# State space angle tables: from GpSimd to VectorE, in ten parts between the remainders of a feed-forward layer

## The reference

```python
def hybrid_layer(x, g_mix, w_in, sinks, w_a, w_b, w_out, g_mlp, w_up, w_down):
    ...
    x = x + mixed @ w_out
    h2 = rmsnorm(x, g_mlp)
    x = x + jnp.square(jax.nn.relu(h2 @ w_up)) @ w_down
    return x

def s5_ssm(u, lam_re, lam_im, log_dt, b_re, b_im, c_re, c_im, d):
    ...
    dt = jnp.exp(log_dt.astype(f32))[:, None]
    mag = jnp.exp(lr * dt)
    ab_re = mag * jnp.cos(li * dt)
    ab_im = mag * jnp.sin(li * dt)
    ...
    _, _, xr, xi = lax.associative_scan(combine, (a_re, a_im, bu_re, bu_im), axis=1)
```

## Time and profile before

| | |
|---|---|
| median of 3 runs | 1128.41 us (1128.15 to 1132.17) |
| the profiled execution, its own time | 1132.87 us |
| its span, first to last instruction | 1131.1 us |
| TensorE matmul busy | 1056.7 us, 93% of the span |
| VectorE busy | 748.0 us, 66% |
| ScalarE busy | 507.5 us, 45% |
| GpSimd busy | 327.7 us, 29% |
| mean granted TensorE clock | 0.968 of full |

### The profile page before, as it was taken

How to read it: one execution, slowest core, us unless ns; L and a number is a source line. 1 busy time by engine, 2 the same in 40 slices (tenths; PEclk the granted TensorE clock), 3 DMA queues, 4 the chain that set the end, 5 groups by cost and what they waited for, 6 DMA issues and landing times.

```text
span 1131.1 us, 15013 instructions
## 1 busy us (share of the span) xinstructions
PE 1056.7 (93%) x6385; PEld 918.7 (81%) x6385; DVE 748.0 (66%) x745; ACT 507.5 (45%) x630; POOL 327.7 (29%) x174
## 2 busy tenths in 40 slices
PE   9899999999999999999999998758999999898687
PEld 7777888898999888777888987747988998897476
DVE  4777646565555557667466677998557584796764
ACT  5355544454444453555444533312457454532242
POOL 0430000000000004300000699997000094284641
PEclk9999999999999999999999998968999999898989
DMA  8444445555655554454454735323645534337222
GB/s 297 145 170 154 150 148 186 161 179 182 195 192 188 176 182 140 168 176 150 149 176 160 223 128 174 107 87 134 221 155 170 186 137 168 103 121 194 76 94 75
DMA packets 97316, 180.34 MB, mean 159 GB/s; under 512 B 8568, under 2 KB 13536, under 8 KB 97120
## 3 DMA queue, kind: packets, MB, share of 16 engines
q1 hardware_dynamic: 97072, 179.28, 48.2%
q10 hardware_dynamic: 176, 0.09, 0.0%
HBM read 175.98 MB, written 1.05 MB: 157 GB/s over the span
## 4 chain that ended last, share of the span: by engine, by line
PE 66%; DVE 17%; DMA 6%; ACT 5%; issue 4%; POOL 2%; SPq 0%; DVEq 0%; POOLq 0%; ACTq 0%
PE bank L677 20%; PE bank L680 19%; PE bank L679 19%; DVE w_lo L1467 9%; DMA raw<-in_w_in 5%; ACT w_hi L1125 4%; DVE arena L1596 2%; PE bank L782 1%; DMA raw<-in_o_w_in 1%; POOL arena L2058 1%; PE bank L1044 1%; PE bank L692 1%; POOL h_sb L2055 1%; PE bank L684 1%; DVE arena L522 1%
## 5 line engine op out<-in xcount | busy, mean ns | idle before, releaser
L1467 DVE TENSOR_TENSOR w_lo<-raw,w_hi 128x2048 fp32r<-128x2048 f32 (+1 forms) x159 | 415.8, 2621 | 272.5 <-ACT w_hi L1125 272.3
L1125 ACT ACTIVATE w_hi<-raw 128x2048 fp32r<-128x2048 f32 (+1 forms) x164 | 310.2, 1892 | 361.2 <-PE bank L680 187.5
L677 PE MATMUL bank<-hT_hi,w_hi 128*128 128x256 f32 x816 | 238.7, 293 | 27.4 <-DVE w_lo L1467 23.2
L679 PE MATMUL bank<-hT_lo,w_hi 128*128 128x256 f32 x792 | 229.0, 289 | 0.0
L680 PE MATMUL bank<-hT_hi,w_lo 128*128 128x256 f32 x792 | 228.9, 289 | 0.0
L677 PE MATMUL bank<-w_hi,hT_hi 128*128 128x512 f32 (+1 forms) x552 | 215.2, 390 | 11.9 <-ACT arena L1137 5.8
L680 PE MATMUL bank<-w_hi,hT_lo 128*128 128x512 f32 (+1 forms) x500 | 192.1, 384 | 0.0
L679 PE MATMUL bank<-w_lo,hT_hi 128*128 128x512 f32 (+1 forms) x500 | 191.8, 384 | 0.0
L677 PEld LDWEIGHTS bank<-hT_hi,w_hi 128*128 128x128 f32 x816 | 162.5, 199 | 32.4 <-DVE w_lo L1467 24.8
L679 PEld LDWEIGHTS bank<-hT_lo,w_hi 128*128 128x128 f32 x792 | 157.4, 199 | 0.4
L680 PEld LDWEIGHTS bank<-hT_hi,w_lo 128*128 128x128 f32 x792 | 156.9, 198 | 0.0
(11 more groups left out here) (299 smaller groups left out, 1237.8 us busy)
## 6 DMA issues: line engine op xcount, KB each, us to landing
raw<-in_w_in SPq DMA_DIRECT2D x44, 1024.0 KB, 5.1
raw<-in_w_up SPq DMA_DIRECT2D x32, 1024.0 KB, 5.3
raw<-in_w_down SPq DMA_DIRECT2D x32, 1024.0 KB, 5.1
raw<-in_e_w_in SPq DMA_DIRECT2D x12, 1024.0 KB, 5.1
raw<-in_o_w_in SPq DMA_DIRECT2D x10, 1024.0 KB, 5.2
raw<-in_w_b SPq DMA_DIRECT2D x8, 1024.0 KB, 5.0
raw<-in_w_out SPq DMA_DIRECT2D x8, 1024.0 KB, 5.1
raw<-in_w_a SPq DMA_DIRECT2D x4, 1024.0 KB, 5.1
```

The lines of the kernel that those rows point to most:

```text
L677: pe.matmul(dst, a_hi, b_hi, start=first, stop=False, skip_group_check=shared)
L679: pe.matmul(dst, a_hi, b_lo, start=False, stop=False, skip_group_check=shared)
L1125: act.activation(w_hi[:, p % SPLIT_RING, :, 0:n], raw[:, p % RAW_RING, :, 0:n], copy).then_inc(hi_ready, 1)
L1467: dve.tensor_tensor(w_lo[:, s, :, 0:n], raw[:, p % RAW_RING, :, 0:n], w_hi[:, s, :, 0:n].bitcast(F32), ALU.subtract).then_inc(lo_ready, 1)
```

## The change

The tables' work leaves GpSimd. `state_space_angles` shrinks to `state_space_turns`, which keeps the small tensors and raises a new semaphore `s5_turns`; it no longer waits for the arena. VectorE gets `state_angles(part)` with ten parts. The tables are made in two halves of 8 tiles (128 x 2048) with five stages each: stage 0 multiplies the time by the high part and finds the whole turns, stage 1 takes them off, stage 2 adds the low part, stage 3 takes whole turns off again, and stage 4 makes the cosine's angle as sin + 0.25 - (sin > 0.25). In groups f = 0 to 4 of the second layer, part 2f stands after the first two remainders of the group and part 2f + 1 after `mlp_square`. ScalarE's two sines move from the second block into groups 5 and 6 of the same layer, where ScalarE waits for both halves (`s5_angles` at 2). VectorE's wait for `s5_angles` ahead of `xg` is gone.

```diff
@@ scalar
                 for f in range(F_GROUPS):
                     step(p + DOWN_PIECE[f])
                     step(p + DOWN_PIECE[f] + 1)
+                    if l == DEPTH - 1 and f in (F_GROUPS - 3, F_GROUPS - 2):
+                        act.wait_ge(s5_angles, 2)
+                        table = (s5_sin, s5_cos)[f - (F_GROUPS - 3)][:, :, :].rearrange("p s t -> p (s t)")
+                        act.activation(table, table, ACT.Sin, scale=TWO_PI).then_inc(s5_tables, 1)
...
             act.activation(s5_small[:, 2, :], s5_small[:, 0, :], ACT.Exp).then_inc(s5_decay, 1)
-            act.wait_ge(s5_angles, 1)
-            act.activation(s5_sin[:, :, :].rearrange("p s t -> p (s t)"), s5_sin[:, :, :].rearrange("p s t -> p (s t)"),
-                           ACT.Sin, scale=TWO_PI).then_inc(s5_tables, 1)
...
-            act.activation(s5_cos[:, :, :].rearrange("p s t -> p (s t)"), s5_cos[:, :, :].rearrange("p s t -> p (s t)"),
-                           ACT.Sin, scale=TWO_PI).then_inc(s5_tables, 1)
@@ vector
+            def state_angles(part):
+
+                half, stage = divmod(part, 5)
+                tiles = range(half * S5_TILES // 2, (half + 1) * S5_TILES // 2)
+                at = slice(tiles[0], tiles[-1] + 1)
+                sin, cos, tmp = (v[:, at, :].rearrange("p s t -> p (s t)") for v in (s5_sin, s5_cos, s5_tmp))
+                order.settle()
+                if stage == 0:
+                    if half == 0:
+                        dve.wait_ge(s5_turns, 1)
+                    for i in tiles:
+                        order.mark(dve.tensor_scalar(s5_sin[:, i, :], tab("time"), s5_small[:, 3, i:i + 1], None, ALU.mult))
+                    order.settle()
+                    order.mark(dve.tensor_scalar(tmp, sin, ROUND, -ROUND, ALU.add, ALU.add))
+                elif stage == 1:
+                    order.mark(dve.tensor_tensor(sin, sin, tmp, ALU.subtract))
+                elif stage == 2:
+                    for i in tiles:
+                        order.mark(dve.scalar_tensor_tensor(out=s5_sin[:, i, :], in0=tab("time"), scalar=s5_small[:, 4, i:i + 1],
+                                                            in1=s5_sin[:, i, :], op0=ALU.mult, op1=ALU.add))
+                elif stage == 3:
+                    order.link(dve.tensor_scalar(tmp, sin, ROUND, -ROUND, ALU.add, ALU.add))
+                    order.mark(dve.tensor_tensor(sin, sin, tmp, ALU.subtract))
+                else:
+                    order.link(dve.tensor_scalar(tmp, sin, 0.25, None, ALU.is_gt))
+                    dve.scalar_tensor_tensor(out=cos, in0=sin, scalar=0.25, in1=tmp, op0=ALU.add, op1=ALU.subtract)\
+                       .then_inc(s5_angles, 1)
+                    dve.wait_ge(s5_angles, half + 1)
...
                 for f in range(F_GROUPS - 1):
                     step(p + DOWN_PIECE[f])
                     step(p + DOWN_PIECE[f] + 1)
+                    if l == DEPTH - 1 and f < 5:
+                        state_angles(2 * f)
                     if f + 2 < F_GROUPS:
                         step(p + UP_PIECE[f + 2])
                         step(p + UP_PIECE[f + 2] + 1)
                         mlp_square(l, f + 2)
+                    if l == DEPTH - 1 and f < 5:
+                        state_angles(2 * f + 1)
...
-                                dve.wait_ge(s5_angles, 1)
@@ gpsimd
-            def state_space_angles():
-
-                pool.wait_ge(out_free[1], (DEPTH - 1) * USES + USE_UP)
+            def state_space_turns():
+
...
-                for i in range(S5_TILES):
-                    order.mark(pool.tensor_scalar(s5_sin[:, i, :], tab("time"), s5_small[:, 3, i:i + 1], None, ALU.mult))
...
-                pool.tensor_tensor(s5_cos, s5_cos, s5_tmp, ALU.subtract).then_inc(s5_angles, 1)
+                pool.tensor_tensor(s[4], s[1], s[3], ALU.subtract).then_inc(s5_turns, 1)
+                pool.wait_ge(s5_turns, 1)
```

More of the change, by code:

```diff
@@ L394, in build_program @@
         s5_decay = sem("s5_decay")
+        s5_turns = sem("s5_turns")
         s5_angles = sem("s5_angles")
```

15 lines of the change are left out of this document (1 added, 14 removed).

## The result

The changed kernel takes **1093.13 us** (median of 4 runs, 1085.92 to 1094.39), the kernel before 1128.28 us beside it (4 runs, 1128.07 to 1132.17). The ratio is 0.967, with a 95% interval of 0.962 to 0.971: faster by 3.3%. The forecast was 1087 us, with a range of 1084 to 1095, of which the forecast's own part is 1084 to 1092.

What follows compares the result with a forecast made beforehand. GpSimd's tables, stalling VectorE and so TensorE in the second layer's feed-forward, were taken as the bound. Removing them gave -41.67 us, VectorE's parts, waits and sines 0: 1128.41 - 41.67 = 1087 us, range 1084 to 1095.

Steps and rivals of the forecast that it cites:

- The bound: Second layer's feed-forward part: GpSimd's tables make it 217.70 us against the first layer's 176.03; removing them gives -41.67 us.
- The cost of the parts: VectorE's added table instructions: 16.5 us per half, 33 us for both, with bounds of 30 and 41 us.
- The cover: VectorE's ten parts in the second layer's feed-forward lie beside other work: cost on the path 0.
- the limit of 6.6 us for a single stop: At the tightest place, in the second sort of part, a single VectorE part shows only beyond 6.6 us.
- So a late remainder does not carry over to the next group: Second layer's feed-forward: after a late remainder and reload, 4.5 us are left, so the next group is not delayed.
- The sines, the waits: ScalarE's two moved sines, in idle time ahead of a group's third `w_hi`, and the semaphore waits: cost 0.
- Rival 1: Ring of weight pieces too tight: parts longer than their idle time delay loads, 13 us in all, 1100 us; chance 0.08.
- Rival 2: The work only changes sides: VectorE's 33 us all lie on the path, clock stays up, 1120 us; chance 0.02.
- Rival 4: Nothing changes, since VectorE is not what stops the second layer: time stays near 1128 us; chance 0.03.
- Rival 3: Slower: parts ahead of awaited remainders expose 41 us and the clock falls, 56.6 us against 41.67 gained, 1143; chance 0.03.
- its price for the clock: Second layer's feed-forward: each us of TensorE idle time costs another 0.38 us through the lower clock.
- so for the median 1128.41 - 41.67: Last step of the sum: the gain taken off the median shown instead of the profiled 1132.87 us, giving 1087 us.

Runs made afterwards that it cites:

- the pieces: Kernel before the change, tables still on GpSimd, each of its eight 128x4096 instructions cut into eight of 128x512: 1102.76 us, second layer's feed-forward part 176.02 us.
- the halves: Kernel before the change, tables still on GpSimd, each 128x4096 instruction cut into two of 128x2048: second layer's feed-forward part 199.26 us.
- the five pairs: Changed kernel with parts 2f and 2f + 1 both behind the squares of group f, five places instead of ten: second layer's feed-forward part 185.11 us.
- the doubled parts: Changed kernel with every instruction of VectorE's ten table parts done twice: second layer's feed-forward part 185.30 us.

## Why the prediction was right

**The bound.** That the 41.67 us were the cost of GpSimd's tables, and all to be had, was right to 0.01 us. That VectorE stood still for the length of one GpSimd instruction was read from a few rows; the pieces and the halves show it.

**The cost of the parts.** The six instructions of 2048 with one input take 1.22 to 1.23 us (taken: 1.17; the 1227 ns of the Trainium skill's page VectorE: DVE Perf Modes, The perf-mode tier table, fit this). scalar_tensor_tensor of 2048 takes 2.29 us (taken: 2.35). Eight tensor_scalar of 256 take 2.19 us, not 2.8: back to back they take 0.27 us each, which the earlier trace rows did not show. VectorE's busy time grows by 127.21 - 96.81 = 30.4 us, predicted 33. (The upper bound of a part, 2.29 + 3.0 = 5.3 us, is written as 5.4; nothing hangs on it.)

**The cover.** Cost 0 on the path was right, and so was the limit of 6.6 us for a single stop (6.5 measured, and 0.65 us lost by one of about 7). The step that failed is the sentence "So a late remainder does not carry over to the next group". It held for the parts as they stand, of 2.3 to 3.5 us, so it did no harm to the forecast. But it did not hold for stops of 5.6 to 7.1 us in each group, which by the limit of 6.6 us for each would have cost about 1 us (0.2 + 0.4 + 0.5) and cost 9.08. The cover is a stock that a group refills only in part.

**The sines, the waits** cost nothing, as taken. Behind the first sine, which ended at 775.13 + 3.63 = 778.76 us, ScalarE still waited 0.77 us for a load, so the sine was not what came last; TensorE idled behind neither.

**The rivals.** Rival 1 (the ring too tight) fell for this placing, but is what the five pairs show. Rival 2, with the rule of the Trainium skill's page Perfetto Trace Analysis (Optimizing Scalar/DVE Operations) that offloading between these two engines "might not help", fell: the move gave back all of the loss. The page says no more than "might not", and here the trace goes the other way: VectorE's busy time fell from 166.05 to 127.21 us with the work added. Rival 4 fell as well: the late loads went with the late remainders (ScalarE waits 23.0 us for loads of `w_down`, 53.3 before). Rival 3 was not met, but its price for the clock was: TensorE's busy time grew by 0.39 us per idle us with the five pairs (178.56 - 176.03 = 2.53 for 185.11 - 178.56 = 6.55) and by 0.41 with the doubled parts, against 0.38 in the prediction; with one long stop it grew by far less (last section).

**The number.** 1093.13 is 6 us above the forecast and above the forecast's own range of 1084 to 1092. It lies inside the stated range only because that takes in half of rival 1, and rival 1 played no part here: that is luck. The mis-sized step is the last one, "so for the median 1128.41 - 41.67". The sum against the profiled execution's own time gave 1091.2; front and tail of the profile after are longer by 3.3 us and its middle is shorter by 0.2, and that makes the 1094.4 that it took. The median shown lay at the low end of what the kernel before takes (later medians 1132.41 to 1134.36), so it was no better a base than the profiled execution. The kernel before took 1128.07 to 1128.41 us in three runs and 1132.17 in a fourth; the step is close to the 5 us between the two tails, but only the execution of 1132.87 us was profiled (long tail, 287.24), so whether the faster ones had the short tail stays open.

## What to carry to other kernels

Before two engines share elementwise work, look at whether the instructions of the one are stretched beside those of the other: if so, either move the work to one of them, or cut the long instructions, which alone gave back all of the 41.67 us in the layer. A busy engine with idle time in every period can take more work, if it is dealt out in pieces well below what the buffers cover: one stop near the limit costs little (0.65 us), the same stop in every period does not (9.08 us for five). Take the sum against the profiled execution, and the scatter of unchanged stretches for the range. Where two engines still start such instructions at almost the same moment, expect two times, by which of them comes first.

## What the runs showed of the hardware that was not expected

One long stop costs little in clock. With all parts at once TensorE idled 26.0 us and its busy time grew by 1.60 us (177.63 - 176.03), 0.06 us per idle us; the halves, with several stops (17.11 us idle), cost 182.15 - 176.03 = 6.12 us, 0.36 per idle us. The windows around the long stop:

```profile
710.00:714.00 4.00, 0.76 (x3) 0.76 (x4) 3.97 (x3) 0.00 (x0) 0.00 (x0) 0.50 0.00 0
714.00:718.00 4.00, 4.00 (x27) 4.00 (x26) 1.39 (x1) 0.00 (x0) 0.00 (x0) 0.71 0.83 296
718.00:722.00 4.00, 4.00 (x36) 4.00 (x35) 1.59 (x1) 1.92 (x1) 0.00 (x0) 1.00 0.63 232
```

The clock is at 0.50 (1.2 GHz) while TensorE idles, where it costs nothing, still low in the window in which TensorE works again (0.71), and at 1.00 (2.4 GHz) in the next. This long stop pays for that return once. That several short ones pay for it each time would explain the difference; it was not tested by itself.

GpSimd is held up as well: an eighth beside VectorE's work takes 2.0 to 2.4 us on average by its line, those of the last line, where VectorE mostly waited for them, 1.27 us each. In the kernel in pieces GpSimd was busy 170.04 us against 153.03.
